# The second half of h made from PSUM on ScalarE, the first half on VectorE

## The reference

```
mod = silu(c) @ w_ada + b_ada ; sh1, sc1, g1, sh2, sc2, g2 = split(mod)
h = rms_norm(x, norm1_g) * (1 + sc1) + sh1
q, k, v, u = split(h @ w_in)            # 512, 128, 128, 512 columns
attn = sliding-window attention of q, k, v (window 128, sinks, partial rotary)
pool = trailing-window means of u (2, 4, 8, 16) minus u, then a linear map per group
x = x + g1 * (concat[attn, pool] @ w_o)
h2 = rms_norm(x, norm2_g) * (1 + sc2) + sh2
x = x + g2 * (relu(h2 @ w_mlp_in)^2 @ w_mlp_out)
```

## Time and profile before

| | us |
|---|---|
| median of three runs | 999.44 |
| lowest and highest run | 994.79, 999.79 |
| the profiled execution: its time | 998.93 |
| its span in the trace | 997.2 |
| TensorE busy | 927.8 (93%) |
| VectorE busy | 684.9 (69%) |
| ScalarE busy | 466.2 (47%) |
| GpSimd busy | 412.6 (41%) |
| the prologue, to the first projection | 0 to 46.3 |
| the eight passes | 46.3 to about 242 |

### The profile page before, as it was taken

The page is one execution under the profiler, slowest core; times in us unless marked ns, Lnnn a source line. Parts: engine busy times, 40 slices in busy tenths (PEclk is TensorE's granted clock), DMA queues, the critical chain, the costliest instruction groups (busy, mean ns, idle before and its releaser), DMA issues.

```text
span 997.2 us, 12512 instructions
## 1 busy us (share of the span) xinstructions
PE 927.8 (93%) x4373; PEld 768.9 (77%) x4373; DVE 684.9 (69%) x1016; ACT 466.2 (47%) x818; POOL 412.6 (41%) x379
## 2 busy tenths in 40 slices
PE   0679999998999999999999979998999999999997
PEld 0668877887778888787887868887887888888886
DVE  4986999987855577665566564544588666779784
ACT  1354655566655554644544535443444444332340
POOL 6444545545433262988788867851000000000001
PEclk9898999999999999999999989999999999999999
DMA  9744332311512350665455433446998728896881
GB/s 328 288 156 146 91 102 84 107 34 51 162 47 83 98 176 11 212 218 171 158 174 193 143 114 138 158 138 213 360 350 302 251 74 260 269 322 197 279 286 54
DMA packets 91982, 174.48 MB, mean 175 GB/s; under 512 B 9288, under 2 KB 26256, under 8 KB 91920
## 3 DMA queue, kind: packets, MB, share of 16 engines
q1 hardware_dynamic: 90704, 173.05, 51.6%
q10 hardware_dynamic: 1216, 0.63, 0.3%
HBM read 135.90 MB, written 37.75 MB: 174 GB/s over the span
## 4 chain that ended last, share of the span: by engine, by line
PE 66%; DVE 15%; DMA 7%; POOL 4%; ACT 4%; issue 2%; SPq 1%; ACTq 0%; POOLq 0%; DVEq 0%
PE psum L1876 21%; PE psum L1878 21%; PE psum L1877 21%; DMA down_raw<-in_w_mlp_out 5%; PE psum L1872 2%; DMA small<-in_attn_sinks 2%; DVE acc L1079 1%; POOL squares L1763 1%; DVE xh L1155 1%; DVE pT_lo L1181 1%; ACT probs L735 1%; DVE down_operands L1598 1%; DVE acc L1374 1%; DVE slots L1192 1%; SPq L590 1%
## 5 line engine op out<-in xcount | busy, mean ns | idle before, releaser
L1876 PE MATMUL psum<-down_operands 128*128 128x512 f32 x448 | 175.5, 392 | 3.9 <-DVE down_operands L1598 3.9
L1878 PE MATMUL psum<-down_operands 128*128 128x512 f32 x448 | 175.0, 391 | 0.0
L1877 PE MATMUL psum<-down_operands 128*128 128x512 f32 x448 | 175.0, 391 | 0.0
L989 ACT CAST down_operands<-down_raw 128x1024 fp32r<-128x1024 f32 x96 | 100.8, 1054 | 156.9 <-PE psum L1878 55.3
L1598 DVE TENSOR_TENSOR down_operands<-down_raw,down_operands 128x1024 fp32r<-128x1024 f32 x93 | 112.2, 1221 | 34.8 <-ACT down_operands L989 33.5
L1864 POOL TENSOR_TENSOR y_second<-y_second,y_first 128x512 f32<-128x512 f32 x3 | 4.2, 1429 | 303.5 <-DVE y_first L1651 303.5
L1876 PE MATMUL psum<-h2T,w_operands 128*128 128x512 f32 x272 | 108.4, 399 | 7.0 <-DVE up_temps L1538 5.1
L1878 PE MATMUL psum<-h2T,w_operands 128*128 128x512 f32 x272 | 106.7, 392 | 0.0
L1877 PE MATMUL psum<-h2T,w_operands 128*128 128x512 f32 x272 | 106.6, 392 | 0.0
L1876 PEld LDWEIGHTS psum<-down_operands 128*128 128x128 f32 x448 | 84.5, 189 | 23.6 <-DVE down_operands L1598 6.2
L1825 POOL TENSOR_TENSOR w_operands<-raw,w_operands 128x512 fp32r<-128x512 f32 x56 | 83.4, 1490 | 42.0 <-ACT w_operands L941 42.0
(11 more groups left out here) (243 smaller groups left out, 1994.9 us busy)
## 6 DMA issues: line engine op xcount, KB each, us to landing
down_raw<-in_w_mlp_out SPq DMA_DIRECT2D x160, 256.0 KB, 4.4
down_raw<-act_scratch SPq DMA_DIRECT2D x112, 256.0 KB, 3.4
raw<-in_w_ada SPq DMA_DIRECT2D x32, 512.0 KB, 4.6
raw<-in_w_mlp_in SPq DMA_DIRECT2D x32, 512.0 KB, 4.9
act_scratch<-act_quads_a SPq DMA_DIRECT2D x64, 256.0 KB, 2.2
act_scratch<-act_quads_b SPq DMA_DIRECT2D x48, 256.0 KB, 3.5
slots<-in_w_ada SPq DMA_DIRECT2D x8, 512.0 KB, 13.1
xh<-in_x SPq DMA_DIRECT2D x8, 512.0 KB, 6.6
```

The lines of the kernel that those rows point to most:

```text
L989: nc.scalar.copy(o[:, 0, :, :], r[:, 0:2, :]).then_inc(op2_hi, 1)
L1876: mm(o, wh, ah, start=first, stop=False, skip_group_check=adds)
L1877: mm(o, wh, al, start=False, stop=False, skip_group_check=adds)
L1878: return mm(o, wl, ah, start=False, stop=last, skip_group_check=adds)
```

## The change

make_h(t) on VectorE makes only blocks 0 to 3 now. Blocks 4 to 7 are made on ScalarE by make_h_half(t), with the activation Identity and a column each as scale and bias. In the loop it stands between the squares of q and hi_pT(t - 2, 0), in the prologue ahead of hi_wu(3). The semaphore h_made is replaced by one for each half, and scale_ready tells ScalarE that both halves of a1 are there; the wait of VectorE on its own last operation of scale_1 goes. pool_windows on TensorE, which overwrites the banks of the turned x, waits for both halves.

```diff
--- before.py
+++ after.py
@@ -272,7 +272,8 @@
 
         x_squared, x_root, x_scaled = sem("x_squared"), sem("x_root"), sem("x_scaled")
         x_turned = sem("x_turned")
-        h_made, h_hi, h_lo = sem("h_made"), sem("h_hi"), sem("h_lo")
+        scale_ready = sem("scale_ready")
+        h_half, h_hi, h_lo = [sem("h_half0"), sem("h_half1")], sem("h_hi"), sem("h_lo")
         u_done, u_kept = sem("u_done"), sem("u_kept")
         band_done, pooled_kept, pout_done, pout_kept = sem("band_done"), sem("pooled_kept"), sem("pout_done"), sem("pout_kept")
         carry_added, carry_kept = sem("carry_added"), sem("carry_kept")
@@ -685,13 +686,25 @@
                 nc.scalar.activation(xh[:, t % 2, :], xh[:, t % 2, :], ACT.Copy,
                                      scale=rx[:, t:t + 1]).then_inc(x_scaled, 1)
 
+            def make_h_half(t):
+
+                if t == 0:
+                    act.wait_ge(scale_ready, 2)
+                act.wait_ge(x_turned, t + 1)
+                for k in range(NK, KD):
+                    ins = nc.scalar.activation(xh[:, t % 2, k * P:(k + 1) * P],
+                                               banks(6 if t == 0 else 1)[:, k * P:(k + 1) * P],
+                                               ACT.Identity, bias=b1[:, k:k + 1], scale=a1[:, k:k + 1])
+                ins.then_inc(h_half[1], 1)
+
             def hi_h(t):
                 if t >= 1:
                     act.wait_ge(kv_done, t)
                 for h in range(2):
                     if t == 0 and h == 1:
+                        make_h_half(0)
                         hi_wu(3)
-                    act.wait_ge(h_made, 2 * t + h + 1)
+                    act.wait_ge(h_half[h], t + 1)
                     nc.scalar.copy(hTh[:, 4 * h:4 * h + 4, :], xh[:, t % 2, 512 * h:512 * h + 512]
                                    .rearrange("p (k n) -> p k n", n=P)).then_inc(h_hi, 1)
 
@@ -787,6 +800,8 @@
                 if t >= 1:
                     act.wait_ge(qk_sums, t)
                 nc.scalar.activation(squares[:, 0:AW], bank(6), ACT.Square).then_inc(q_squared, 1)
+                if t + 1 < NT:
+                    make_h_half(t + 1)
                 if t >= 2:
                     hi_pT(t - 2, 0)
                 act.wait_ge(kv_done, t + 1)
@@ -1144,17 +1159,17 @@
                 own_d.step(v.tensor_tensor(a1[:, c4], a1[:, c4],
                                            cols[:, 8 * SC1 + 4 * h:8 * SC1 + 4 * h + 4], ALU.add))
                 own_d.wait()
-                own_d.step(v.scalar_tensor_tensor(out=a1[:, c4], in0=a1[:, c4], scalar=1.0,
-                                                  in1=cols[:, 48 + 4 * h:52 + 4 * h], op0=ALU.add, op1=ALU.mult))
-                own_d.wait()
-
-            def make_h(t, h):
-                if h == 0:
-                    dve.wait_ge(x_turned, t + 1)
-                for k in range(4 * h, 4 * h + 4):
+                v.scalar_tensor_tensor(out=a1[:, c4], in0=a1[:, c4], scalar=1.0, in1=cols[:, 48 + 4 * h:52 + 4 * h],
+                                       op0=ALU.add, op1=ALU.mult).then_inc(scale_ready, 1)
+
+            def make_h(t):
+                if t == 0:
+                    dve.wait_ge(scale_ready, 1)
+                dve.wait_ge(x_turned, t + 1)
+                for k in range(NK):
                     ins = v.tensor_scalar(xh[:, t % 2, k * P:(k + 1) * P], banks(6 if t == 0 else 1)[:, k * P:(k + 1) * P],
                                           a1[:, k:k + 1], b1[:, k:k + 1], ALU.mult, ALU.add)
-                ins.then_inc(h_made, 1)
+                ins.then_inc(h_half[0], 1)
 
             def lo_h(t, h):
                 dve.wait_ge(h_hi, 2 * t + h + 1)
@@ -1163,10 +1178,9 @@
                                 hTh[:, 4 * h:4 * h + 4, :].bitcast(F32), ALU.subtract).then_inc(h_lo, 1)
 
             scale_1(0)
-            make_h(0, 0)
+            make_h(0)
             scale_1(1)
             lo_h(0, 0)
-            make_h(0, 1)
             lo_h(0, 1)
             for k in range(KD):
                 a = landed(dve, ("wqkv", k))
@@ -1301,11 +1315,9 @@
                                                      in1=acc[:, k * P:(k + 1) * P], op0=ALU.mult, op1=ALU.add)
                     ins.then_inc(gate_biased, 1)
                 if t + 1 < NT:
-                    make_h(t + 1, 0)
+                    make_h(t + 1)
                 if t >= 2:
                     lo_pT(t - 2, 0)
-                if t + 1 < NT:
-                    make_h(t + 1, 1)
                 dve.wait_ge(q_squared, t + 1)
                 dve.wait_ge(kv_squared, t + 1)
                 v.tensor_reduce(ssq, squares[:, 0:AW + KVW]
@@ -1985,7 +1997,8 @@
                 if t < 2:
                     pe.wait_ge(consts_made, t + 1)
                 if t + 1 < NT:
-                    pe.wait_ge(h_made, 2 * (t + 2))
+                    for h in range(2):
+                        pe.wait_ge(h_half[h], t + 2)
                 else:
                     pe.wait_ge(qk_lo, t)
                 for j in range(NP):
```

## The result

| | us |
|---|---|
| changed kernel, median of 20 runs (lowest to highest) | 1000.13 (998.57 to 1002.21) |
| kernel before, median of 20 runs beside them | 997.24 (994.79 to 1000.52) |
| ratio, with its 95% interval | 1.0032 (1.0023 to 1.0041) |
| profiled execution of the changed kernel: time, span | 1002.21, 1000.5 |

By the ratio the change costs 3.2 us (2.3 to 4.1). The three runs of before from which the forecast took its level had a high median, 999.44 against 997.24 over twenty. So "999.6" came within 0.5 us of the measured median by luck: the level was 2.2 us too high and the change about 3 us too cheap.

A forecast was written before the change was run, and what follows sets the result against it. The round trip over TensorE and ScalarE was taken to bound passes 3 to 6. Terms of -0.2 (passes) and +0.4 (prologue) gave +0.2 us: 999.1 for the profiled execution, 999.6 as the median, range 994.5 to 1001.5.

The forecast's parts named there:

- The bound: Passes 3 to 6: lo_pT(t-2, 1) waits for turn_p and hi_pT; VectorE has only 0.06 us of its own to give.
- VectorE's follow-up time: Pass 7, which makes no h: lo_pT starts 0.62 us after hi_pT; applied to pass 5, it gives 187.84.
- The term of the passes: Passes 3 to 6: VectorE's freed time gains 0.06 us a pass, -0.2 us; the rest becomes idle time before lo_pT(t-2, 1).
- The prediction's slack of 0.3 us in pass 2: Pass 2: lo_pT(0, 0) ends at 108.9 with the moved work on ScalarE, and TensorE asks for it at 109.27.
- B: Before lo_pT(t-2, 0): four ACTIVATE take 2.9 us, ScalarE becomes late; 1.1 us in pass 2, 5.2 us overall, 1004.6; chance 0.04.
- ScalarE's cost: Passes 0 to 6, ahead of hi_pT(t-2, 0): four added ACTIVATE take 1.49 us, free under some 1.8 us.
- ScalarE's lateness in the prologue: Prologue: hi_h(0, 1) ends at 47.8 against 47.41, delaying the casts of W_qkv; +0.4 us on the path, bounds 0 and +0.75.
- the second part of the prologue: Prologue: lo_wu(3) ends near 49.8, lo_h(0, 1) at 48.9, both just in time; value 0, bounds 0 and +0.3.
- the prediction's sign for "right": Prologue: turn_x(1) at 57.7 to 57.9, the first cast of W_qkv 0.3 to 0.5 us later.
- A: Passes 3 to 6: VectorE's time is the path, so the whole 1.3 us arrives; -4.8 us, 994.6; chance 0.10.
- C: First projection: TensorE runs dry between k = 4 and k = 6, its clock falls, 1.9 us; 1001.3 to 1001.5; chance 0.06.
- D: The work that follows settles otherwise than in the profiled run, as in one run with 994.79; chance 0.10.

The follow-up runs named there:

- f1: Kernel before, except that in the passes nobody makes the second half of h (tiles 1 to 7 take scaled x there); 997.35 us, ratio 1.0008.
- e3: Changed kernel with both halves of h back on VectorE in the passes, so only the prologue is changed; 998.50 us, ratio 1.0013 to before.
- e4: Kernel before with only hi_wu(3) held until VectorE has made the second half of h of tile 0; 1000.10 us, ratio 1.0028 to before.
- f3: e2 with ScalarE making the second half of h twice in each pass; 1000.09 us, ratio 1.0042 to the kernel before.
- e2: Changed kernel with the prologue's second half back on VectorE and hi_wu(3) at its old place; 997.48 us, ratio 1.0006 to before.
- e1: Changed kernel with hi_wu(3) ahead of the second half of h of tile 0 on ScalarE; 999.52 us, ratio 1.0027 to before.
- h1: The kernel of e1 run once more; 998.61 us, ratio 1.0016 to the kernel before.
- h3: The reordered passes of h4 with the prologue of e1; 996.08 us, ratio 0.9983 to the kernel before.
- h2: The kernel of e2 run once more; 998.21 us, ratio 1.0004 to the kernel before.
- h4: e2 with hi_pT(t-2, 0) and lo_pT(t-2, 0) ahead of the halves of h on ScalarE and VectorE; 994.13 us, ratio 0.9972 to before.

## Why the prediction was right in sign and wrong in size

**The bound.** Right. The round trip over TensorE and ScalarE sets lo_pT(t - 2, 1), and VectorE's follow-up time read off pass 7, 0.62 us, is what pass 5 shows now: 188.43 to 189.05. f1 bears it out without any ScalarE work.

**The term of the passes,** -0.2 us: measured -0.3, but not from where I had it, so this agreement is luck. The whole difference lies between turn_x(5) and turn_x(6), 25.47 before, 25.14 after, and it is in e3 too, whose passes are those of before. It goes with the order in which VectorE and GpSimd meet once. Timelines of VectorE, then GpSimd, in the kernel before:

```profile
154.66 2.33 DVE L1077 TENSOR_SCALAR acc<-raw,small 128x1024 f32<-128x1024 f32 x1 [0.19 <-issue]
157.03 1.28 DVE L1079 SCALAR_TENSOR_TENSOR acc<-raw,small,acc 128x1024 f32<-128x1024 f32 x1
...
154.56 1.90 POOL L1721 TENSOR_TENSOR probs<-probs,small 128x1024 f32<-128x1024 f32 x1 [2.01 <-DVE small L1224]
```

and in the changed one:

```profile
155.93 0.76 DVE L1092 TENSOR_SCALAR acc<-raw,small 128x1024 f32<-128x1024 f32 x1
156.72 2.79 DVE L1094 SCALAR_TENSOR_TENSOR acc<-raw,small,acc 128x1024 f32<-128x1024 f32 x1
...
156.08 2.36 POOL L1733 TENSOR_TENSOR probs<-probs,small 128x1024 f32<-128x1024 f32 x1 [2.00 <-DVE small L1238]
```

Before, GpSimd was first and VectorE's 0.76 us operation ended 0.53 us behind it; afterwards VectorE was first, and its pair of operations ended 0.3 us earlier, counted from turn_x(5). All fourteen profiles fall in line: GpSimd was first in before and in e4, both with 25.47; VectorE was first in the other twelve. What decides who comes first wasn't tried. The 0.06 us per pass in passes 3 to 6 is too small to be seen. (The prediction's slack of 0.3 us in pass 2 comes to 0.4 us by its own terms, 109.27 - 108.87; only B's 1.1 us in pass 2 hangs on it, and f3 made that pass 1.3 us longer than e2 did.)

**ScalarE's cost.** Right: 1.50 us for four against 1.49 from the h2 rows. By the formula of the Trainium skill (VectorE: DVE Perf Modes, section on the TRN2 errata) the move would be even. The traces do not agree: four take 1.35 us on VectorE and 1.50 on ScalarE.

**ScalarE's lateness in the prologue,** +0.4 us: the first cast of W_qkv starts 5.23 us behind the first half of h, before 4.93: +0.30. Right, but it never reached the path as a term of its own; it lies beneath the next one.

**The step that failed** is the second part of the prologue: lo_wu(3) and lo_h(0, 1) "just in time", a stall of 0.1 to 0.4 us absorbed, "Value 0, bounds 0 and +0.3". I gave lo_h(0, 1) the 1.00 us of its row "beside GpSimd" as if that were its speed there. The row says something else: 47.54 + 1.00 = 48.54 is 0.55 us behind GpSimd's 47.99. Read so, my own estimates would have given 49.8 + 0.54 = 50.3 for its end and not 48.9, 1.2 us behind TensorE's k = 4 at 49.13, and 1.8 us behind 48.54 for the start of the eight low parts of W_qkv on VectorE, with GpSimd's root behind them. Measured for turn_x(1): +1.85 us in one profile of the changed kernel, +2.9 with the clock in the other, where the prediction's sign for "right" was 57.7 to 57.9, +0.25 to +0.45. Nor had TensorE anything to absorb a stall with: its row for turn_x(1) shows no idle time before it, and in e3, where turn_x(1) waited for TensorE alone, k = 4 came at 7.98 in place of 6.65 us behind the first half of h and turn_x(1) at 16.29 in place of 14.97, 1.3 us later both times. I looked at ScalarE's queue as the only way to turn_x(1) and left out VectorE's and GpSimd's.

The Trainium skill has this as a rule (SBUF — State Buffer, section "SBUF: two separate sides"): VectorE and GpSimd have one pair of ports in common, held exclusively for a whole instruction by whichever comes first, when VectorE's operation has two SBUF inputs and GpSimd's reads SBUF too; the other waits. The rows above agree, 0.54 us from GpSimd's end to VectorE's. It would have been a rival on the slower side, with a price of 1.8 us by the rows.

**The rivals.** A is out by f1, B's price by the 1.50 us and its mechanism seen in f3. C I had at 0.06, with a stall that "would have to be far longer than 0.4 us"; the stall was 1.50 and 1.93 us, and the clock fell behind the second and cost 1.0 us where C had 1.9. D: the level of three runs was high by 2.2 us.

**What stays open.** Up to turn_x(7) the profiled delay is +1.85 - 0.3 = 1.6 us, or 2.6 with the clock, leaving out turn_x(1) to turn_x(2), which takes 25.3 to 26.6 us over the profiles (26.12 before, 26.51 changed) without pattern. Measured over the runs are 3.2 and 3.8, so 1.2 to 1.6 us have no place in a profile. e1, h1 and h3 stay above e2, h2 and h4 by a similar amount, 1.1 to 2.1 us, which speaks for the second half of tile 0 on ScalarE. But e3 has that half on ScalarE too and costs 1.3 us where its trace shows 1.0, and e4, without it, costs 2.8 us where its trace shows 1.9, both with intervals of 2.6 us. So the assignment is not shown. Each profile is one execution besides: the changed kernel's is the slowest of its twenty, e1's the fastest of its twelve. The wait dropped from scale_1 and the doubled wait of pool_windows weren't tried alone.

## What to carry to other kernels

When work is put ahead of a step in one engine's queue, follow that step through every engine it feeds: here the price was not the 1.5 us moved, but a cast that let GpSimd's subtraction start 1.9 us later and hold VectorE's until it ended. Where an operation's row is longer than its like, compare its end with the end of the neighbour's before taking the duration as a price. And when a busy engine turns out to lie inside a round trip over others, don't lighten it; start the round trip earlier. Here lightening gave nothing and the earlier start 2.3 us over the passes, though it was tried only with the second half already on ScalarE.

## What the runs showed of the hardware that I had not expected

- A VectorE operation with two SBUF inputs that starts while GpSimd works on SBUF ends 0.54 to 0.56 us behind GpSimd's, wherever it began: 1.00 to 2.55 us for an operation of 0.69 us, in fourteen profiles. An operation of 1.28 us, held in the same way, ended 1.07 us behind it (the row at 156.72). One with a single tensor input in SBUF, the TENSOR_SCALAR of 128x1024, was held too: 2.33 us in place of 0.76, with its end 0.53 us behind GpSimd's (the row at 154.66).
- It holds the other way too, but not always: GpSimd's root on 128x1 took 2.09 us beside a train of VectorE's two-input operations and ended 0.07 us behind the train; in e3 and e4 the same root took 0.36 and 0.33 us in the middle of the train, and the next GpSimd operation 1.15 us in place of 0.57.
- The four tensor_scalar from PSUM on VectorE beside the same GpSimd operation kept their 1.36 us (before, 45.49 to 46.85).
- With the same code TensorE's granted clock stayed at 1.00 behind an idle time of 1.50 us, and fell (0.71 over 4 us) behind one of 1.93 us. In the first profile it had risen from 0.50 only some 4 us before the idle time; in the second it had been at 1.00 since 20 us at least. Which of the two differences counts is not shown.
